# A hybrid attention trunk: new matmul tiles and a new order in the even mixer, and a new order around three other places

## The chip, the core and the metric

The kernel runs on one NeuronCore of a Trainium2 chip. The metric is the device time of one execution in microseconds (us). Before the change it is 1285.05 us, the median of three runs (1284.8, 1285.05 and 1287.28). Lower is better. TensorE is called PE here, VectorE DVE, ScalarE ACT, GpSimd POOL and SyncE SP.

## The reference

Two post-norm residual layers on x of 512 tokens by 1024 features, float32 throughout. The even layer runs gated linear attention (GLA, 4 heads) and local attention (8 query heads, 2 key heads, 64 features each) side by side. The odd layer is gated DeltaNet. Each mixer and each SwiGLU block is followed by a layer norm.

```python
def _even_mixer(x, w_in, w_a2, b_a, gla_norm_g, sinks, w_out):
    h = x @ w_in
    gq, gk, gv, ga, gr, sq, sk, sv = _split_cols(h, EVEN_WIDTHS)
    o = jnp.concatenate([_gla(gq, gk, gv, ga, gr, w_a2, b_a, gla_norm_g),
                         _swa(sq, sk, sv, sinks)], -1)
    return o @ w_out

# _swa: chunks of 64 tokens, each sees itself and the chunk before it
    sc = jnp.einsum('bcikgd,bcjkd->bckgij', qc, kw).astype(f32) * (SWA_HEAD_DIM ** -0.5)
    sc = jnp.where(valid[None, :, None, None, None, :], sc, -jnp.inf)
    ...
    p = jax.nn.softmax(jnp.concatenate([sc, sink], -1), axis=-1)[..., :-1]
    o = jnp.einsum('bckgij,bcjkd->bcikgd', p.astype(vw.dtype), vw)

# _gla, per chunk: attention within the chunk plus a state carried on
    attn = jnp.where(causal, jnp.einsum('bhcid,bhcjd->bhcij', q_g, k_g), 0.0)
    o_intra = jnp.einsum('bhcij,bhcjv->bhciv', attn, vc)
        o_c = jnp.einsum('bhid,bhdv->bhiv', q_c, state)
        state = state * jnp.exp(bl_c)[..., None] + jnp.einsum('bhjd,bhjv->bhdv', k_c, v_c)
    ...
    o = _norm_no_affine(o) * norm_g * jax.nn.silu(r)

# every sub-layer
    x = _layer_norm(ALPHA * x + mix, ln1_g[layer], ln1_b[layer])
```

## The kernel before, in words

Tokens are worked in four tiles of 128 (`NT` = 4, index t). All engines run hand-written programs, and their order is the order of the code. They meet by semaphores. The eight PSUM banks are handed out by `unit_plan`, which walks the list of all matmul units in PE's order and gives each the next bank of a ring. A unit waits in `fill` until the last user of its bank has `take`n the result.

Large products are split. A weight or an activation is rounded by ACT to a high part (`w_hi`, `x_hi`), and the rest (`w_lo`, `x_lo`) is subtracted by POOL or DVE. Each product then is three matmuls in fp32r (`mm3`, lines 1562 to 1564). Weights come in blocks of 1 MB through two buffers: SP loads one, ACT rounds it (`split_to`, line 768), POOL makes the low part (`split_lo`, line 638). The small products of the mixers are plain fp32, where one matmul is recorded as two passes.

In the even mixer, PE does for each tile t: scores of the local attention (line 1782, 64 tokens of a chunk by 128 keys, with keys padded by zeros to 128 features), two transposes of the decayed GLA keys (`kd`), the whole projection tile `gr` (24 matmuls of 512 columns), GLA products (`gattn` line 1794, `gstate` line 1771, `gout` lines 1762 and 1808), transposes of the probabilities (`probT`, line 1815), the local output (`sout`, line 1824), and transposes of the concatenated output of the tile before (`oT`, line 1695). DVE takes the maximum of the scores, subtracts it and writes `s_p` (line 1247). ACT takes the exponential of `s_p` (line 880), DVE sums it and scales the output. After the four tiles come tiles of the output projection, `mix`, of which two are placed ahead of the last `oT` (`TAIL_FILLERS`).

After each layer norm, `turn_x` (line 1680) transposes the normalised x into eight banks. DVE scales each bank into `f_ab` (line 1083), ACT rounds it (line 775), DVE and POOL in turn make `x_lo` (lines 1075 and 645). The first weight block behind it is walked with `fresh` set: for each k, two output banks, three matmuls each, after `x_lo` of k has come.

The odd layer convolves 24 channel blocks (`CONV_ORDER`, on DVE at line 1355) and then runs the delta rule over the four tiles. Projection tiles (`FILLERS`) are set between the small products. Its outputs are scaled by DVE (`out_scale`) and multiplied by the gate on POOL (`gate_output`, line 678) before they are turned.

## Time and profile before

| what | before |
|---|---|
| median of 3 runs | 1285.05 us |
| the profiled execution: its time, its span | 1283.91 us, 1282.1 us |
| PE busy, matmuls recorded | 1250.3 us (98%), 7104 |
| DVE, ACT, POOL busy | 462.7, 432.9, 598.9 us |
| mean DMA rate | 96 GB/s |
| even mixer's four tiles, PE | 94.39 to 159.80 us |

The span is the stretch between the first and last record, and the time of the execution lies 1.8 us above it. A busy engine is not always an engine at its peak: records of matmuls overlap, so the distance from one start to the next tells more than the length of one. Idle time is written in brackets behind a row, with the engine that ended it.

### The profile page before, as it was taken

What the parts mean: (1) busy time and instruction counts of PE and PEld (TensorE: products, weight loads), DVE (VectorE), ACT (ScalarE), POOL (GpSimd) and SP (SyncE); (2) the same over time, 40 slices, a digit from 0 to 9 for tenths busy, and PEclk for the clock granted to TensorE, in tenths of its full rate; (3) what the DMA queues carried; (4) which work ended last, traced back from release to release, by engine and by line L of the source; (5) the groups of instructions that cost most, each with busy time, mean ns of one, the idle gap of its engine ahead of it and who ended that gap; (6) DMA issues with size and microseconds to landing.
All of it is one profiled execution on the core that took longest, in us unless ns stands there. A gap on an engine that the chain in (4) does not pass through costs nothing.

```text
span 1282.1 us, 16970 instructions
## 1 busy us (share of the span) xinstructions
PE 1250.3 (98%) x7104; PEld 1027.5 (80%) x7104; DVE 462.7 (36%) x763; ACT 432.9 (34%) x600; POOL 598.9 (47%) x286
## 2 busy tenths in 40 slices
PE   9999999999999999998999999999999999999997
PEld 7878877888888888886777878887788888888885
DVE  5548945211111000115687955553521101010105
ACT  4174623322222221224453355452422222221111
POOL 4241243964444443445743346364595444435341
PEclk9999999999999999999999999999999999999999
DMA  9321032333333233231344342022233333324221
GB/s 305 99 67 66 1 115 84 99 99 99 98 99 99 83 121 125 99 96 49 98 110 124 99 100 92 26 67 99 66 99 99 99 99 99 99 82 134 80 99 65
DMA packets 109375, 122.98 MB, mean 96 GB/s; under 512 B 22386, under 2 KB 84148, under 8 KB 109300
## 3 DMA queue, kind: packets, MB, share of 16 engines
q1 hardware_dynamic: 101828, 118.59, 29.4%
q10 hardware_dynamic: 7472, 3.31, 1.0%
q8 instruction: 56, 0.92, 0.3%
q14 instruction: 19, 0.16, 0.0%
HBM read 117.96 MB, written 3.70 MB: 95 GB/s over the span
## 4 chain that ended last, share of the span: by engine, by line
PE 86%; DVE 7%; POOL 3%; issue 3%; DVEq 1%; ACT 1%; ACTq 0%; POOLq 0%
PE bank L1562 26%; PE bank L1563 26%; PE bank L1564 26%; PE bank L1893 3%; POOL w_lo L638 2%; DVE f_ab L1083 1%; DVE KH L1355 1%; DVE OO L1333 1%; DVE SS L1331 1%; PE bank L1608 1%; DVEq L435 1%; PE bank L1721 0%; PE bank L1845 0%; DVE x_tm L1106 0%; PE bank L1782 0%
## 5 line engine op out<-in xcount | busy, mean ns | idle before, releaser
L638 POOL TENSOR_TENSOR w_lo<-w_raw,w_hi 128x1024 fp32r<-128x1024 f32 (+1 forms) x200 | 470.0, 2374 | 495.3 <-ACT w_hi L768 495.3
L1562 PE MATMUL bank<-x_hi,w_hi 128*128 128x512 f32 x928 | 364.3, 393 | 7.5 <-DVE f_ab L1083 4.0
L1564 PE MATMUL bank<-x_hi,w_lo 128*128 128x512 f32 x928 | 361.7, 390 | 0.0
L1563 PE MATMUL bank<-x_lo,w_hi 128*128 128x512 f32 x928 | 361.6, 390 | 0.0
L768 ACT ACTIVATE w_hi<-w_raw 128x1024 fp32r<-128x1024 f32 (+1 forms) x200 | 196.3, 1031 | 218.3 <-issue 167.3
L1562 PEld LDWEIGHTS bank<-x_hi,w_hi 128*128 128x128 f32 x928 | 174.6, 188 | 46.9 <-issue 8.4
L1564 PEld LDWEIGHTS bank<-x_hi,w_lo 128*128 128x128 f32 x928 | 174.5, 188 | 36.6
L1563 PEld LDWEIGHTS bank<-x_lo,w_hi 128*128 128x128 f32 x928 | 174.5, 188 | 35.4
L1150 DVE TENSOR_TENSOR f_ab<-bank,f_ab 128x512 f32<-128x512 f32 x44 | 30.4, 691 | 368.9 <-PE bank L1564 368.9
L1563 PE MATMUL bank<-w_lo,h_hi 128*128 128x512 f32 x352 | 140.4, 399 | 0.0
L1562 PE MATMUL bank<-w_hi,h_hi 128*128 128x512 f32 x352 | 138.7, 394 | 0.0
L1564 PE MATMUL bank<-w_hi,h_lo 128*128 128x512 f32 x352 | 138.0, 392 | 0.0
L1562 PE MATMUL bank<-w_hi,x_hi 128*128 128x512 f32 (+1 forms) x320 | 124.3, 388 | 3.6 <-POOL w_lo L638 2.1
L1564 PE MATMUL bank<-w_hi,x_lo 128*128 128x512 f32 (+1 forms) x320 | 121.5, 380 | 0.0
L1563 PE MATMUL bank<-w_lo,x_hi 128*128 128x512 f32 (+1 forms) x320 | 121.3, 379 | 0.0
L1141 DVE SCALAR_TENSOR_TENSOR x_tm<-x_tm,bank 128x512 f32<-128x512 f32 x32 | 22.0, 687 | 260.9 <-PE bank L1564 259.7
L803 ACT ACTIVATE h_hi<-f_ab 128x512 fp32r<-128x512 f32 x44 | 27.8, 633 | 189.0 <-DVE f_ab L1150 189.0
L1562 PEld LDWEIGHTS bank<-w_hi,h_hi 128*128 128x128 f32 x352 | 66.1, 188 | 17.2
L1564 PEld LDWEIGHTS bank<-w_hi,h_lo 128*128 128x128 f32 x352 | 66.1, 188 | 15.8
L1563 PEld LDWEIGHTS bank<-w_lo,h_hi 128*128 128x128 f32 x352 | 66.1, 188 | 15.2
L798 ACT ACTIVATE f_ab<-bank 128x512 f32<-128x512 f32 x44 | 26.4, 600 | 144.1 <-PE bank L1564 143.9
L1562 PEld LDWEIGHTS bank<-w_hi,x_hi 128*128 128x128 f32 x320 | 60.2, 188 | 16.5 <-POOL w_lo L638 3.4
(270 smaller groups left out, 1179.5 us busy)
## 6 DMA issues: line engine op xcount, KB each, us to landing
w_raw<-ffn_w_gate_dram SPq DMA_DIRECT2D x22, 1024.0 KB, 5.3
w_raw<-ffn_w_up_dram SPq DMA_DIRECT2D x22, 1024.0 KB, 5.3
w_raw<-ffn_w_down_dram SPq DMA_DIRECT2D x20, 1024.0 KB, 5.0
w_raw<-od_w_in_dram SPq DMA_DIRECT2D x16, 1024.0 KB, 5.9
w_raw<-ev_w_in_dram SPq DMA_DIRECT2D x8, 1024.0 KB, 5.9
w_raw<-ev_w_out_dram SPq DMA_DIRECT2D x4, 1024.0 KB, 5.1
w_raw<-od_w_out_dram SPq DMA_DIRECT2D x4, 1024.0 KB, 5.1
x_fm<-x_fm_dram SPq DMA_DIRECT2D x8, 256.0 KB, 6.7
```

Of the source, the lines that this page charges most:

```text
L435: e.drain()
L638: pool.tensor_tensor(w_lo[:, b % 2, c], w_raw[:, b % 2, c], w_hi[:, b % 2, c].bitcast(F32), ALU.subtract).then_inc(w_lo_ready, 1)
L768: act.activation(w_hi[:, i % 2, c], w_raw[:, i % 2, c], ACT.Copy).then_inc(w_hi_ready, 1)
L798: take(act.activation(f_ab[:, j, :], bank(("gate", layer, f + j))[:, :], ACT.Silu), ("gate", layer, f + j))
L803: act.activation(h_hi[:, f + j, :], f_ab[:, 2 + j, :], ACT.Copy).then_inc(s["h_hi_ready"], 1)
L1083: take(dve.tensor_scalar(f_ab[:, k % 4, :], src, lnc[:, gcol + k:gcol + k + 1], lnc[:, gcol + 16 + k:gcol + 17 + k], ALU.mult, ALU.add), ( ...
L1141: take(dve.scalar_tensor_tensor(cols, cols, ALPHA, bank(key)[:, :], ALU.mult, ALU.add), key)
L1150: take(dve.tensor_tensor(f_ab[:, 2 + f % 2, :], bank(("up", layer, f))[:, :], f_ab[:, f % 2, :], ALU.mult), ("up", layer, f))
L1562: pe.matmul(out_ap, st[0], mv_[0], start=start, stop=False)
L1563: pe.matmul(out_ap, st[0], mv_[1], start=False, stop=False)
L1564: return pe.matmul(out_ap, st[1], mv_[0], start=False, stop=stop)
L1893: return pe.matmul(o, a, b_, start=True, stop=True)
```

## The change

Even mixer. Even query heads lie on partitions 0 to 63 and odd ones on 64 to 127, so the scores are products of 64 features in four 64 by 64 tiles of the array, into two banks (index e is the parity of the head). Keys are no longer padded with zeros: they are written twice, and two transposes per tile do what four did. ACT takes the exponential straight from the bank, with the maximum as bias, and its sum output gives the denominators; that is eight instructions of 128 columns in place of two of 512 on `s_p`. POOL multiplies the probabilities by the inverse sums. The local output is computed by features (`windowed`), so it needs no transpose. `gattn` is computed only within chunks, `gout` from it in 64-row tiles, and the state of two heads is updated by one DVE instruction. Mean and variance come from `bn_stats`. Probabilities of tile t are turned and used in tile t+1, between parts of `gr`, and the last tiles of `mix` are interleaved with them.

Elsewhere. Normalised x is signalled in halves; the `fresh` block starts with the matmuls that need only `x_hi`; POOL makes the first half of the next weight block before the low parts of x. The first two convolutions no longer restart the ring of banks, and the copy of `ba_fm` moves from DVE to ACT. In the odd layer the transposes at the start take other banks, a filler goes ahead of `vTM`, `qk` goes ahead of the small blocks, the blocks' DRAM scratch is laid out in two planes, and the last output is scaled and gated by one DVE instruction per head, with the fillers around it reordered.

```diff
+EVEN_FILLERS = [[("gr", t)] for t in range(NT)]
+LAST_FILLERS = {0: [("mix", 0, 0, 2)], 1: []}
+def turned(layer, t, i):
+    return ("sout", t) if (layer, i) == (0, 1) else ("oT", layer, t, i)
@@ unit_plan
-        u += [("score", t, 0), ("score", t, 1), ("kd", t), ("gr", t), ("gattn", t), ("gstate", t, 0), ("gout", t),
-              ("gstate", t, 1), ("probT", t, 0), ("probT", t, 1), ("sout", t)]
+        u += [("score", t, 0), ("score", t, 1), ("kd", t)] + EVEN_FILLERS[t]
         if t:
-            u += [("oT", 0, t - 1, 0), ("oT", 0, t - 1, 1)]
+            u += [("probT", t - 1, 0), ("probT", t - 1, 1), ("oT", 0, t - 1, 0), ("sout", t - 1)]
+        u += [("gattn", t), ("gstate", t, 0), ("gout", t), ("gstate", t, 1)]
-        if key == ("conv", CONV_ORDER[0]):
+        if key == ("ba_fm",):
             ring, turn = list(range(6)), 0
-            ring, turn = [0, 1, 2, 3, 6, 7, 4, 5], 0
+            ring, turn = [0, 6, 7, 1, 2, 3, 4, 5], 0
+        elif key[0] == "gstate" and key[2] == 1 and key[1]:
+            b = slots["probT", key[1] - 1, 0][0]
@@ SP: the odd layer's blocks
-        t_dram = nc.dram_tensor("t_blocks", (P, SB, 2, SB), F32).ap()
+        t_dram = nc.dram_tensor("t_blocks", (2, P, SB, SB), F32).ap()
@@ POOL
+                        pool.wait_ge(s["s_den_ready"], t + 1)
+                        for e in range(2):
+                            p = s_p[:, t % 2, e, :].rearrange("p (h n) -> p h n", h=4)
+                            den = s_den[:, t % 2, e:QH:2].unsqueeze(2).broadcast_to([P, 4, P])
+                            pool.tensor_tensor(p, p, den, ALU.mult).then_inc(s["s_weight"], 1)
                 if b in turned:
+                    pool.wait_ge(s["z_norm"], 2 * NT * turned[b])
+                    split_lo(b + 1, (0,))
                     low_parts(turned[b])
@@ ACT: even tile
+                if t:
+                    copy_probs(t - 1)
-                    act.activation(s_p[:, g, :], s_p[:, g, :], ACT.Exp).then_inc(s["s_prob"], 1)
+                    for j in range(4):
+                        h = 2 * j + e
+                        ins = act.activation(s_p[:, t % 2, e, j * P:(j + 1) * P], bank(("score", t, e))[:, j * P:(j + 1) * P],
+                                             ACT.Exp, bias=s_max[:, h:h + 1], scale=HD ** -0.5,
+                                             accum_out=s_den[:, t % 2, h:h + 1])
@@ DVE: layer norm
-                    dve.tensor_scalar(x_tm[:, t, :], x_tm[:, t, :], mv[:, t, 0:1], rstd[:, t:t + 1],
-                                      ALU.subtract, ALU.mult).then_inc(s["z_norm"], 1)
+                    for h in range(2):
+                        c = slice(h * 512, (h + 1) * 512)
+                        dve.tensor_scalar(x_tm[:, t, c], x_tm[:, t, c], mv[:, t, 0:1], rstd[:, t:t + 1],
+                                          ALU.subtract, ALU.mult).then_inc(s["z_norm"], 1)
@@ DVE: even tile
-                    take(dve.scalar_tensor_tensor(heads4(s_p[:, g, :]), k4(key), HD ** -0.5,
-                                                  across(s_max[:, hs], P), ALU.mult, ALU.subtract), key)
@@ DVE: last output of the odd layer
-                out_scale(NT - 1, hg)
+                for h in range(4 * hg, 4 * hg + 4):
+                    ins = dve.scalar_tensor_tensor(OO[:, h, :], OO[:, h, :], oms[:, h:h + 1],
+                                                   gate_s[:, NT - 1, h * P:(h + 1) * P], ALU.mult, ALU.mult)
@@ PE: fresh block
+                for k in range(KD) if fresh is not None else ():
+                    weights_there(b, k)
+                    pe.wait_ge(s["x_hi_ready"], KD * fresh + k + 1)
+                    x = xcols(k, ALL)
+                    for n in range(len(keys)):
+                        pe.matmul(ps[:, :], w[0], x[0], start=k == 0, stop=False)
+                        pe.matmul(ps[:, :], w[1], x[0], start=False, stop=False)
+                    low_part_there(pe, fresh, k)
@@ PE: even tile
-                            ins = pe.matmul(ps[c * CH:(c + 1) * CH, hh * P:(hh + 1) * P],
-                                            s_qT[:, h // 2, chunk * CH:(chunk + 1) * CH],
-                                            s_kT[:, 2 * g + h % 2, chunk * CH:chunk * CH + 2 * CH],
+                            ins = pe.matmul(ps[e][c * CH:(c + 1) * CH, j * P:(j + 1) * P],
+                                            s_qT[dims, j, chunk * CH:(chunk + 1) * CH],
+                                            s_kT[dims, j // 2, chunk * CH:chunk * CH + 2 * CH],
                                             start=True, stop=True)
-                tile_of(("gr", t))
+                tile_of(gr, 0, 3)
+                if t:
+                    turn_probs(t - 1)
+                    turn_o(0, t - 1)
+                tile_of(gr, 3, 6 if t < NT - 1 else 8)
+                if t:
+                    windowed(t - 1)
...
+            for k0 in (0, 2):
+                for key in TAIL_FILLERS[0]:
+                    tile_of(key, k0, k0 + 2)
+            turn_probs(NT - 1)
+            for key in TAIL_FILLERS[0]:
+                tile_of(key, 4, 6)
+            windowed(NT - 1)
```

On PE, an even tile before read like this, from its scores to the next tile's (the rows of `gr` and of `sout` that repeat are left out):

```order
L1782 MATMUL bank<-s_kT,s_qT 64x128 x16
L1789 MATMUL bank<-eye,g_kd 128x128 x2
...
L1794 MATMUL bank<-q_pad,g_k 128x128 x4
L1771 MATMUL bank<-g_v,g_kdt 64x128 x4
L1762 MATMUL bank<-g_S,q_pad 64x128 x4
...
L1808 MATMUL bank<-g_v,g_at 128x128 x4
L1815 MATMUL bank<-eye,s_p 128x128 x8
L1824 MATMUL bank<-s_vsh,s_pT 64x64
L1824 MATMUL bank<-s_v,s_pT 64x64
...
L1695 MATMUL bank<-eye,o_tm 128x128 x8
```

And after, for tile 1, where the dots stand for parts of `gr` (9, 9 and 6 matmuls) and for repeats:

```order
L1864 MATMUL bank<-s_kT,s_qT 64x128 x16
L1872 MATMUL bank<-eye,g_kd 128x128 x2
...
L1829 MATMUL bank<-eye,s_p 128x128 x8
L1756 MATMUL bank<-eye,o_tm 128x128 x4
...
L1842 MATMUL bank<-s_pT,s_vsh 64x2x64 x2
L1842 MATMUL bank<-s_pT,s_v 64x2x64 x2
...
L1886 MATMUL bank<-q_pad,g_k 64x64 x8
L1853 MATMUL bank<-g_v,g_kdt 64x128 x4
L1820 MATMUL bank<-g_S,q_pad 64x128 x4
...
L1906 MATMUL bank<-g_v,g_at 64x128 x8
```

The probabilities and the local output of the tile before now stand inside `gr`, half of the transposes of `o_tm` are gone, and `gattn` and the product with `g_at` come in eight matmuls of 64 rows out.

On ACT, an even tile before:

```order
L875 ACTIVATE g_kdt<-bank 128x256
L879 ACT_TABLE_LOAD
L879 ACTIVATE s_snk<-s_snk 128x4
L880 ACTIVATE s_p<-s_p 128x512
...
L882 ACT_TABLE_LOAD
L882 ACTIVATE g_r<-bank 128x512
L887 ACTIVATE s_pT<-bank 128x512 x2
L891 ACT_TABLE_LOAD
L891 ACTIVATE g_var<-g_var,eps 128x4
```

And after, tile 2, with its waits:

```order
L901 ACTIVATE s_pT<-bank 128x512 [waits bank_full4]
L901 ACTIVATE s_pT<-bank 128x512 [waits bank_full5]
L911 ACT_TABLE_LOAD
L911 ACTIVATE s_snk<-s_snk 128x4 [waits s_shift]
L919 ACTIVATE s_p,s_den<-bank,s_max 128x128 [waits bank_full0,s_weight,s_den_ready,bank_full1]
L919 ACTIVATE s_p,s_den<-bank,s_max 128x128 x3
L911 ACTIVATE s_snk<-s_snk 128x4 [waits bank_taken0,s_shift]
L919 ACTIVATE s_p,s_den<-bank,s_max 128x128 [waits bank_full1,s_weight,s_den_ready,bank_full2]
...
L930 ACT_TABLE_LOAD
L930 ACTIVATE g_r<-bank 128x512 [waits bank_full3]
```

The copies of the probabilities moved ahead of the exponentials, and the exponentials now hold the two score banks (0 and 1 in this tile) until they end. `gattn` and the first `gstate` of the tile are given the same two banks.

On PE, the first block behind a layer norm, before (the second one, in front of the convolutions) and then after:

```order
L1562 MATMUL bank<-x_hi,w_hi 128x512 [waits bank_taken0,x_lo_even,w_lo_ready]
L1563 MATMUL bank<-x_lo,w_hi 128x512
L1564 MATMUL bank<-x_hi,w_lo 128x512
L1562 MATMUL bank<-x_hi,w_hi 128x512 [waits bank_taken1]
```

```order
L1642 MATMUL bank<-x_hi,w_hi 128x512 [waits bank_taken6,x_hi_ready,w_lo_ready]
L1643 MATMUL bank<-x_hi,w_lo 128x512
L1642 MATMUL bank<-x_hi,w_hi 128x512 [waits bank_taken7]
L1643 MATMUL bank<-x_hi,w_lo 128x512
L1646 MATMUL bank<-x_lo,w_hi 128x512 [waits x_lo_even]
L1646 MATMUL bank<-x_lo,w_hi 128x512
L1642 MATMUL bank<-x_hi,w_hi 128x512 [waits x_hi_ready]
```

The matmuls with the low part of x stand last in each k, and a wait for the high part has taken the place of the first one.

## Rows read from the trace of the kernel before

**Rows 1.** The page: busy time of PE.
```profile
PE 1250.3 (98%) x7104; PEld 1027.5 (80%) x7104; DVE 462.7 (36%) x763; ACT 432.9 (34%) x600; POOL 598.9 (47%) x286
```

**Rows 2.** Waits of PE: engine, line, releaser: total us, times, longest us.
```profile
PE bank L1562 <- DVE f_ab L1083: 4.0, 2, 3.5
...
PE bank L1934 <- DVE KH L1355: 3.2, 1, 3.2
PE bank L1562 <- POOL w_lo L638: 2.1, 2, 1.1
...
PE bank L1893 <- DVE GA L1462: 1.6, 3, 0.5
...
PE bank L1782 <- ACT g_v L870: 0.9, 1, 0.9
```

**Rows 3.** Timeline of PE, even tile 1: start us, length us, instruction, records.
```profile
109.95 1.92 PE L1782 MATMUL bank<-s_kT,s_qT 128*64 128x128 f32 x32
111.80 0.44 PE L1789 MATMUL bank<-eye,g_kd 128*128 128x128 f32 x2
...
117.58 1.05 PE L1794 MATMUL bank<-q_pad,g_k 128*128 128x128 f32 x8
118.56 0.65 PE L1771 MATMUL bank<-g_v,g_kdt 64*64 64x128 f32 x8
119.14 1.09 PE L1762 MATMUL bank<-g_S,q_pad 128*64 128x128 f32 x8
...
123.01 1.04 PE L1815 MATMUL bank<-eye,s_p 128*128 128x128 f32 x8
...
125.59 1.09 PE L1695 MATMUL bank<-eye,o_tm 128*128 128x128 f32 x8
126.61 0.33 PE L1782 MATMUL bank<-s_kT,s_qT 128*64 128x128 f32 x2
```

**Rows 4.** Timeline of PE, odd layer: products in 32 by 32 tiles.
```profile
759.26 0.69 PE L1893 MATMUL bank<-blocks_in,GA 32*32 32x32 f32 x32
```

**Rows 5.** Timeline of ACT and DVE: nearest rows to the new instructions.
```profile
846.76 2.53 ACT L1009 ACTIVATE GT<-GT,ndec 128x128 f32<-128x128 f32 x8 [2.89 <-POOL GT L698]
849.31 1.28 ACT L993 ACT_TABLE_LOAD   x1
...
855.78 1.13 DVE L1502 SCALAR_TENSOR_TENSOR qkv<-bank,nbexp,qkv 128x128 f32<-128x128 f32 x4
...
126.10 0.69 DVE L1284 TENSOR_TENSOR r_tmp<-o_tm 128x512 f32<-128x512 f32 x1
...
159.19 1.28 DVE L1280 TENSOR_SCALAR g_mu<-g_mu 128x4 f32<-128x4 f32 x1
```

**Rows 6.** Timeline, behind the first and the second layer norm.
```profile
212.57 0.63 ACT L775 ACTIVATE x_hi<-f_ab 128x512 fp32r<-128x512 f32 x1 [0.84 <-DVE f_ab L1083]
...
214.14 0.47 PE L1562 MATMUL bank<-x_hi,w_hi 128*128 128x512 f32 x1 [1.69 <-DVE x_lo L1075]
...
582.15 0.63 ACT L775 ACTIVATE x_hi<-f_ab 128x512 fp32r<-128x512 f32 x1 [0.84 <-DVE f_ab L1083]
...
585.58 0.47 PE L1562 MATMUL bank<-x_hi,w_hi 128*128 128x512 f32 x1 [3.55 <-DVE f_ab L1083]
...
589.76 0.39 PE L1562 MATMUL bank<-x_hi,w_hi 128*128 128x512 f32 x1
```

**Rows 7.** Busy time by stretch; the eighth figure is the granted clock.
```profile
586.90:589.50 2.60, 2.44 (x6) 1.95 (x7) 1.92 (x4) 1.26 (x2) 1.32 (x2) 0.50 0.00 0
```

**Rows 8.** Timeline: the odd layer's constants on ACT's queue, and their use.
```profile
601.36 0.34 ACTq L934 DMA_DIRECT2D o_own<-c_small_dram  x1
...
607.86 0.51 PE L1867 MATMUL bank<-o_eye,ba_fm 128*128 128x16 f32 x4
```

**Rows 9.** Timeline of POOL: in the even mixer's last tile, and the last gate products.
```profile
155.74 9.86 POOL L638 TENSOR_TENSOR w_lo<-w_raw,w_hi 128x1024 fp32r<-128x1024 f32 x4
...
871.27 2.89 POOL L678 TENSOR_TENSOR OO<-OO,gate_s 128x512 f32<-128x512 f32 x2 [16.44 <-DVE OO L1436]
```

More of the change, by code:

```diff
@@ L871, in _, with copy_probs @@
             split_to(first_block[("gr",)] + 1)
+            def copy_probs(t):
+                for g in range(KVH):
+                    full(act, ("probT", t, g))
+                    take(act.activation(s_pT[:, g, :], bank(("probT", t, g))[:, :], ACT.Copy), ("probT", t, g))
             for t in range(NT):
@@ L1259, in _ @@
                     v = 2 * t + c
[L1260 to L1266 removed]
+                    col = (2 * t + c + 1) * CH - 1
@@ L1699, in have @@
                 def have(k):
[L1700 to L1703 removed]
+                    taken(pe, turned(layer, NT - 1, k // 4))
+                tm_group(("mix", layer, 1), have, in_turn=True)
                 turn_x(2 * layer + 1)
```

340 lines of the change are left out of this document (189 added, 151 removed).

## The prediction, made blind

> **What bounds the kernel now.** I read the page first: PE is busy for 98% of the span, the other engines for half of it or less [rows 1]. So only PE's queue counts: instructions taken out of it, a stretch in which it ran slowly, or a wait of its own. Another engine costs something only where PE waits for it. The list of PE's waits comes second. The ones that this change touches are short: 4.0 and 2.1 us before line 1562, 3.2 us for `KH`, 1.6 us for `GA`, 0.9 us for `g_v` [rows 2]. Third, I read the timeline of even tile 1, start to start, since lengths overlap [rows 3]. The tile takes 126.61 - 109.95 = 16.66 us. Scores take 1.85 (to 111.80). `kd` and the 24 matmuls of `gr` take 5.78 (to 117.58), so about 0.23 a matmul. `gattn` takes 0.98 and the first four `gstate` matmuls 0.58. From 119.14 to 123.01 lie 3.87 of GLA products with one wait, then 2.58 of `probT`, a wait for its copy, and `sout`, and 1.02 of `oT`. A group of four fp32 matmuls of 128 columns (8 records) takes 0.98: I read that as 4 x 0.213 plus 0.13 for the change of shape. `gstate`, which uses two column halves at once, costs 0.58 for the same count, half of 0.85 plus 0.13. A transpose is one record: `probT`'s eight and `kd`'s two give 0.10 to 0.11 each.
>
> **The even mixer, PE alone.** The new tile holds these parts. Scores: 16 matmuls. If the four 64 by 64 tiles run side by side they need 16 x 0.213 / 4 + 0.13 = 0.98; if only two do, today's 1.85. The trace has no 64 by 64 fp32 product in four tiles, so these are the bounds. The nearest row is the odd layer's products in 32 by 32 tiles: 32 records (16 matmuls of 32 columns, 16 x 0.053 + 0.13 = 0.98 in series) were over in 0.69 [rows 4], so tiles of different rows do overlap. I take 1.0. `kd` stays at 0.19, and `gr` costs 5.59 plus two more changes of shape, 5.85. `probT` 0.98. `oT` with four transposes in place of eight: 0.43 plus no change of shape behind `probT`. `windowed` 8 matmuls of 128 columns by halves, 0.98. `gattn` in chunks, eight of 64 columns by halves, 0.56, `gstate` 2 x 0.58, the products with `g_S` 2 x 1.02, `g_v` by `g_at` in eight 64-row matmuls 0.98. The sum is 14.2, against 16.66.
>
> The last term has a dissenter. Rows 4 show two row tiles going into one bank and overlapping, 0.69 against 0.98. The Trainium skill, "TensorEngine Tiling (Array Packing)", section Restrictions and Gotchas, says: "Different row tiles cannot access same PSUM bank simultaneously". By it the eight matmuls would stand in a row, 8 x 0.213 + 0.13 = 1.83, or 0.85 more in each tile and 3.4 in the four; the forecast would be 1269.4. The scores keep the rule, since each row half has its own bank.
>
> **The even mixer, the other engines.** PE will not reach 14.2, because `oT` and the scores' banks now hang on DVE and ACT. After a tile's last product DVE does its statistics, four scalings of 128 columns from a bank (1.13 for four of that kind) and a product of 512 columns (0.69) [rows 5]; with `bn_stats` on four heads, which I price like four more of 128 columns, and small operations (0.17 when nobody disturbs, 1.28 at worst, beside POOL's `w_lo` [rows 5]) `o_tm` is ready some 5.2 us into the next tile. PE, after scores, `kd`, 9 matmuls of `gr` and `probT`, wants it at about 4.4. Wait: 0.8. ACT copies the probabilities of the tile before until about 5.3, loads a table (1.28), and does eight exponentials at 2.53 / 8 = 0.32 [rows 5]: they end at about 9.6. `gattn` and the first `gstate` take the two score banks, which are only free then, and PE is there at about 9.3. That is another 0.3. The new tile is therefore 14.2 + 0.8 + 0.3 = 15.3, a gain of about 1.35 in tiles 1 and 2.
>
> Tile 0 starts 1.06 earlier, since nothing waits for `g_v` any more (0.9 in [rows 2], the rest the change of shape), and it carries neither `probT` nor `windowed` nor `oT`: 2.58 + 1.0 go out (3.37 of these 3.6 come back behind tile 3), with 0.5 to 0.6 saved by `gattn` and half the scores. I put tile 1's start at 105.0 instead of 109.95, which after the part that only moves leaves 1.6. With 1.35 twice and a little more for tile 3, whose scores and `gattn` give 1.3 as well, that is 7 us at its end. From there the tail counts: today PE resumes about 31.6 behind tile 3's start. Its pace is POOL's there, 9.86 / 4 = 2.47 per `w_lo` of 1024 columns [rows 9], for which PE already waits 1.1 at its longest [rows 2]; the change adds two products of 512 columns (about 1.25 each) to POOL in this place and `probT` and `windowed` to PE, covered by two `mix` tiles. I add 0.4. The even mixer so comes to **-6.5**, by the gains alone -9.4 at most, and 0 if each tile runs at the old pace. Two transposes of keys in each tile go away with the second half of `s_kT`, 8 x 0.106 in all: **-0.85**.
>
> **Layer norms.** Behind the first, PE starts at 214.14, while `x_hi` of k = 0 ended at 212.57 + 0.63 = 213.20 [rows 6]. The new order needs only that: -0.9, and 0.2 more since the next low part no longer holds it: **-1.1**. The third behaves alike: **-1.1**. Behind the second it is more. `x_hi` ended at 582.78, PE started at 585.58 (a bank of the ring was held by `f_ab`, 3.55 of idle time), then ran with a granted clock of 0.50, the lower level, in which six matmuls took 2.60 instead of 1.4 [rows 7], after a stretch in which it had been idle; the tenth matmul began at 589.76 [rows 6]. With the ring no longer restarted PE begins at about 582.8 at full clock and its tenth matmul is at about 585.0: -4.8. What is late next is the constants: ACT issues their load at 601.36 and PE uses them at 607.86, 6.5 behind [rows 8]; the use moves to about 602.9, and I let PE wait 1.3. **-3.5**, between 0 (if the whole of it waits for the load) and -4.8.
>
> **The odd layer.** The wait for `KH`, 3.2, falls away as the first transposes take banks whose users are long done; for this the scratch blocks must land 3 us earlier, and they are now written in long runs. The three waits for `GA`, 1.6, have `qk` placed in front. At the end POOL's two gate products, 2.89 [rows 9], leave the path; DVE does them per head with the scaling, four and four of 0.28, where it did a scaling of 0.69 twice: 0.8 more on DVE for 2.89 less on POOL, of which 1.1 reaches PE, since fillers cover the rest. **-5.9**, between -1 and -6.5.
>
> **Sum.** 6.5 + 0.85 + 1.1 + 1.1 + 3.5 + 5.9 = 18.95. The profiled execution took 1283.91 (span 1282.1 and 1.8 around it), which gives 1265.0. The median of the runs shown, 1285.05, is 1.1 above it, so I forecast **1266**. All terms at their good end give 1285.05 - (9.4 + 0.85 + 2.4 + 4.8 + 6.5) = 1261; with half of the even gain and half of the odd one it is about 1272, and with one more such loss 1274: own range 1261.5 to 1274.
>
> **Rivals.**
> A: the even mixer gains nothing. A tile is as long as the loop over DVE, ACT and the two shared banks. For it: POOL's new products stand on the same engine as `w_lo` (2.47 each), and a single small DVE operation has cost 1.28 beside it; four such make the loop 16.7. Or the scores need 1.85 and the sums a copy more. Against it: DVE and ACT are busy for a third of the span, and DVE's chain from the bank loses its passes of 0.69 over `s_p`. Then 6 go: 1272.
> B: the odd layer's loads set the time. If blocks or constants land no earlier, 3.2 of the `KH` wait stands again as a DMA wait, and the norm's gain shrinks by 0.5 more: 1269.7. For it: PE's need moves forward by 3 us and the issue doesn't. Against: the writes leave earlier too.
> C, slower: the sum output of the exponential. No row shows an exponential with one. It could cost a separate read behind each instruction, and 0.65 us more on each of 32 makes the ACT chain of a tile 8 x 0.65 = 5.2 longer. Since PE waits for the last exponential at `gattn`, all but nothing of that is covered: 4 x 5.2 = 21 turns 1266 into 1287. It decides from 19 / 32 = 0.6 on. If it is 0.3, the tile grows 2.4 and the result is about 1275. For it: eight outputs in place of none. Against: the nearest row, eight activations of this size, runs at 0.32 each with nothing between.
> D: all tiles at PE's own pace of 14.2, no wait for `o_tm`: 1.1 less in each of three, and the constants land in time: 1261.5.
>
> **Chances.** Forecast 0.58, A 0.22, B 0.10, C 0.05 (0.04 of it above 1282), D 0.05. My range for 8 times in 10 is 1259 to 1277: it takes in D with its bounds, A, B and the mild form of C. About 0.2%, 2.6 us, is what a measurement of this kernel can tell from no change. Faster by more 0.93; within it 0.03, which needs A with C's mild form and B; slower 0.04, C in full.
>
> **What the profile after would show.** Scores of a tile within about 1.0 us (wrong: 1.85). From one tile's scores to the next's 15.3 (A: 16.6; D: 14.2), with PE waiting for `o_tm` at line 1756 and for ACT at `gattn`. An exponential with sum at 0.32 (C: about 1.0, or an extra record behind each). The group of `g_v` by `g_at` at 0.98 (the quoted rule: 1.8). The first matmul behind the first and third layer norm 0.9 earlier relative to `x_hi`. Behind the second a granted clock of 1.0 and a start with `x_hi`; a wait for the constants' load at the product with `ba_fm`, 1.3 at most. No wait for `KH`; if one for a DMA is there, B. The forecast is wrong as a whole if even tiles are 16 us or longer, or if a wait of over 3 us appears in the odd layer that [rows 2] do not have.

## The result, and the profile after

The changed kernel takes 1275.43 us (median of four runs, 1275.22 to 1279.39); the kernel before, with one more run beside them, 1286.09. The ratio is 0.9925, 95% interval 0.9902 to 0.9948. The change is a gain of some 10 us, where 19 were forecast: 1275.4 against 1266, inside the stated range and outside the forecast's own (1261.5 to 1274). The profiled execution took 1275.52 us, its span is 1273.7.

The first look is at the same two views as before. The page:

```profile
PE 1241.7 (97%) x7080; PEld 1020.2 (80%) x7080; DVE 439.2 (34%) x768; ACT 440.6 (35%) x657; POOL 605.2 (48%) x292
```

PE is still the bound, but it is busy for 8.6 us less than in [rows 1] and the span is 8.4 shorter. So as much idle time came in as went out. The waits of PE say where (engine, line, releaser: total us, times, longest):

```profile
PE bank L1608 <- DVE KH L1398: 5.4, 1, 5.4
PE bank L1853 <- ACT s_p L919: 3.7, 3, 1.4
PE bank L1608 <- POOL w_lo L655: 3.1, 3, 2.5
PE bank L1642 <- ACT x_hi L799: 2.9, 3, 1.0
PE bank L1608 <- DVE x_lo L1138: 1.5, 2, 0.7
...
PE bank L1886 <- ACT s_p L919: 1.0, 2, 0.6
PE bank L1756 <- DVE OO L1581: 0.9, 2, 0.5
```

The waits of [rows 2] for `f_ab`, for `GA` and for `g_v` are gone. A wait for `KH` is there, but not the old one: it stands before line 1608, a large matmul of a convolution. Three others are new, two for the exponentials `s_p` and one for `x_lo` in front of line 1608. The wait for `x_hi`, 2.9 in all at the three norms, stands where one for `x_lo` was before (3.4 in all at two of them).

A table by stage follows, read from the starts of single matmuls in the two timelines (us). The rest of the analysis goes by it.

| stage of PE | before | after | measured | forecast |
|---|---|---|---|---|
| start to first scores | 94.39 | 93.95 | -0.44 | with the next |
| even mixer, to the first turn of x | 113.26 | 112.24 | -1.02 | -7.35 for both |
| first norm and up projection | 246.37 | 245.85 | -0.52 | -1.1 |
| down projection | 123.21 | 120.86 | **-2.35** | 0 |
| second norm, to the product with `ba_fm` | 30.63 | 26.58 | -4.05 | -3.5 |
| convolutions, to the first `kTM` | 134.00 | 138.28 | **+4.28** | -3.2 |
| delta rule, output projection | 161.80 | 160.12 | -1.68 | -2.7 |
| third norm and up projection | 246.37 | 245.88 | -0.49 | -1.1 |
| down projection | 123.36 | 121.01 | **-2.35** | 0 |

Three places are off, in both directions: the even mixer, the convolutions, and two stages in which the diff changes nothing.

**The convolutions.** The timelines of PE and then of DVE around the new wait:

```profile
655.51 0.46 PE L1935 MATMUL bank<-qkv 128*32 128x32 f32 x32
661.40 0.80 PE L1608 MATMUL bank<-x_hi,w_hi 128*128 128x512 f32 x1 [5.43 <-DVE KH L1398]
661.99 0.63 PE L1609 MATMUL bank<-x_lo,w_hi 128*128 128x512 f32 x1
```
```profile
650.28 1.28 DVE L1439 TENSOR_SCALAR ssq<-ssq 128x32 f32<-128x32 f32 x1
...
651.98 1.94 DVE L1441 TENSOR_TENSOR beta<-beta,rk 128x32 f32<-128x32 f32 x1
...
655.25 1.28 DVE L1450 TENSOR_TENSOR GT<-GT,nbeta 128x512 f32<-128x512 f32 x2
656.62 4.72 DVE L1398 SCALAR_TENSOR_TENSOR KH<-bank,convw,KH 128x511 f32<-128x511 f32 x6
```

DVE works through a list of small operations and comes only at 656.62 to the two convolutions that PE has finished last (three instructions each). PE wants the bank of the second of them at once, and gets it at 661.34. After that its granted clock is down to the lower level, 0.59 of full speed on average over 5.6 us (the eighth figure):

```profile
661.40:667.00 5.60, 5.60 (x15) 4.50 (x16) 0.00 (x0) 0.10 (x1) 3.92 (x2) 0.59 0.13 16
```

The 24 large matmuls behind the wait take 7.80 where the neighbouring groups of 24 take 5.66, so the wait costs 5.43 + 2.14 = 7.6 us. Why there, `unit_plan` tells. The ring of six banks now starts at `ba_fm`, two units later than before, so the twelfth convolution of `CONV_ORDER` gets bank 0. The thirteenth restarts the ring of four, and gets bank 0 too. Before, the twelfth had bank 2.

**Even tiles.** PE at the start of tile 1, in its middle, and at the start of tile 2 (the two records of a product are counted apart, and a few stand in rows of their own that are left out):

```profile
105.13 0.97 PE L1906 MATMUL bank<-g_v,g_at 64*64 64x128 f32 x13
...
106.00 1.09 PE L1864 MATMUL bank<-s_kT,s_qT 64*64 64x128 f32 x30
107.03 0.44 PE L1872 MATMUL bank<-eye,g_kd 128*128 128x128 f32 x2
...
114.44 0.69 PE L1886 MATMUL bank<-q_pad,g_k 128*64 128x64 f32 x16 [0.38 <-ACT s_p L919]
116.44 0.65 PE L1853 MATMUL bank<-g_v,g_kdt 64*64 64x128 f32 x8 [1.32 <-ACT s_p L919]
...
122.10 1.09 PE L1864 MATMUL bank<-s_kT,s_qT 64*64 64x128 f32 x30
123.13 0.44 PE L1872 MATMUL bank<-eye,g_kd 128*128 128x128 f32 x2
124.30 0.50 PE L1608 MATMUL bank<-w_hi,x_hi 128*128 128x512 f32 x1 [0.74 <-DVE x_lo L1138]
```

The products themselves cost what was forecast: scores 1.03 (1.0), `g_v` by `g_at` in 64-row tiles 0.87 up to the scores (0.98; 1.02 in e6, where another shape follows), in one bank, on different halves of its partitions, and side by side; in series they would have been 1.7 to 1.83. So the dissenting term of the prediction, 1.83 by the quoted rule, did not come: this measurement decides against it. But tile 1 is 16.10 long and tile 2 17.39 (forecast 15.3, and 16.66 in [rows 3]), with waits for the exponentials of 1.7 and 2.1 where I had 0.3 (0.9 in tile 3), and in tiles 2 and 3 one of 0.74 for `x_lo` in front of `gr`, which I had not at all. Behind tile 3 PE waits 2.48 for POOL's `w_lo`, and the granted clock over the next 3.0 us is 0.53:

```profile
154.39 1.09 PE L1906 MATMUL bank<-g_v,g_at 64*64 64x128 f32 x16
157.96 0.77 PE L1608 MATMUL bank<-w_hi,x_hi 128*128 128x512 f32 x1 [2.48 <-POOL w_lo L655]
```

On ACT a read of the accumulator stands behind each exponential, 0.345 from one exponential to the next:

```profile
112.88 0.37 ACT L919 ACTIVATE s_p<-bank,s_max 128x128 f32<-128x128 f32 x1
113.14 0.19 ACT L919 ACTIVATION_READ_ACCUMULATOR s_p<-bank,s_max 128x1 f32 x1
113.24 0.36 ACT L919 ACTIVATE s_p<-bank,s_max 128x128 f32<-128x128 f32 x1
```

**Down projection.** The first matmul of the stage and the one behind its last, before and then after:

```profile
454.02 0.39 PE L1562 MATMUL bank<-w_hi,h_hi 128*128 128x512 f32 x1
...
577.23 0.27 PE L1680 MATMUL bank<-eye,x_tm 128*128 128x128 f32 x1
```
```profile
452.04 0.39 PE L1608 MATMUL bank<-w_hi,h_hi 128*128 128x512 f32 x1
...
572.90 0.27 PE L1742 MATMUL bank<-eye,x_tm 128*128 128x128 f32 x1
```

The same 528 matmuls, with no wait inside, start every 0.2333 us before and every 0.2289 after. The instructions are the same. The granted clock is 1.00 in both. What moved is their data: the even mixer's small buffers grew by 32 bytes in each partition, and everything allocated behind them, h included, now starts at a multiple of 64 bytes instead of 32 beyond one. That this is the cause is not shown by these rows; e1, e2 and others below try it.

### The profile page after: what moved, and what is told of

It is laid out like the page before. It is cut to its first block, busy times and chain, and to the rows that moved or that the text cites. A ratio compares the mean times of both kernels' runs of the same rounds, so it can differ in the third digit from the quotient of the medians.

```text
span 1273.7 us, 17029 instructions
## 1 busy us (share of the span) xinstructions
PE 1241.7 (97%) x7080; PEld 1020.2 (80%) x7080; DVE 439.2 (34%) x768; ACT 440.6 (35%) x657; POOL 605.2 (48%) x292
## 4 chain that ended last, share of the span: by engine, by line
PE 89%; DVE 5%; ACT 2%; POOL 2%; DVEq 1%; issue 1%; ACTq 0%; POOLq 0%
PE bank L1608 27%; PE bank L1609 26%; PE bank L1610 26%; PE bank L1983 3%; POOL w_lo L655 1%; PE bank L1646 1%; DVEq L449 1%; PE bank L1642 1%; PE bank L1643 1%; DVE stats L1190 1%; ACT s_p L919 1%; DVE x_tm L1188 1%; DVE x_tm L1161 1%; PE bank L1667 1%; PE bank L1780 1%
## 5 line engine op out<-in xcount | busy, mean ns | idle before, releaser
L1608 PE MATMUL bank<-x_hi,w_hi 128*128 128x512 f32 x880 | 345.3, 392 | 5.4 <-DVE KH L1398 5.4
L1609 PE MATMUL bank<-x_lo,w_hi 128*128 128x512 f32 x880 | 343.3, 390 | 0.0
L1610 PE MATMUL bank<-x_hi,w_lo 128*128 128x512 f32 x880 | 343.2, 390 | 0.0
L1608 PEld LDWEIGHTS bank<-x_hi,w_hi 128*128 128x128 f32 x880 | 165.7, 188 | 40.9 <-DVE KH L1398 5.5
L1610 PEld LDWEIGHTS bank<-x_hi,w_lo 128*128 128x128 f32 x880 | 165.7, 188 | 34.5
L1609 PEld LDWEIGHTS bank<-x_lo,w_hi 128*128 128x128 f32 x880 | 165.8, 188 | 34.2
L1610 PEld LDWEIGHTS bank<-w_hi,h_lo 128*128 128x128 f32 x352 | 66.1, 188 | 14.8
```

The source lines that it names most:

```text
L1608: pe.matmul(out_ap, st[0], mv_[0], start=start, stop=False)
L1609: pe.matmul(out_ap, st[0], mv_[1], start=False, stop=False)
L1610: return pe.matmul(out_ap, st[1], mv_[0], start=False, stop=stop)
```

## The experiments

They were timed in four groups, each beside the kernel before, whose median there was 1285.25, 1285.08, 1285.07 and 1284.95.

**e3, the ring of the convolutions.**

```diff
         elif key == ("conv", CONV_ORDER[BLOCKS_AT]):
-            ring, turn = list(range(4)), 0
+            ring, turn = [1, 2, 3, 0], 0
         elif key == FILLERS[0, -1]:
-            ring, turn = [0, 6, 7, 1, 2, 3, 4, 5], 0
+            ring, turn = [1, 6, 7, 2, 3, 0, 4, 5], 0
```

> The changed kernel with one thing different: the ring of four banks for the last twelve convolutions starts at bank 1 and not at 0 (and the ring behind it is turned the same way). In the changed kernel conv 11 and conv 12 in order both have bank 0, and PE waits 5.4 us there and then runs at the lower clock for a while. Theory R (ring collision): the wait goes, the 7.6 us lost between the 12th and the 13th convolution come back, about 1268. Rival (DVE bound): DVE's queue of small operations in front of conv 11 is what is late; PE then waits one or two convolutions later for another bank, and less than 2 us are gained.

Measured: 1267.21 us (1267.1 to 1267.68), ratio to before 0.9858 [0.9842, 0.9873]. The stage from `ba_fm` to `kTM` goes from 138.28 to 130.65, 7.63 less, and no other stage moves by more than 0.1; the start to the first scores, which the edit doesn't touch, varied by 0.8 between these two executions and gives the rest. Behind the same small products PE now goes on at once:

```profile
654.77 0.46 PE L1935 MATMUL bank<-qkv 128*32 128x32 f32 x32
655.16 0.50 PE L1608 MATMUL bank<-x_hi,w_hi 128*128 128x512 f32 x1
```

DVE's list was no shorter, and PE waits for none of it later. So the cause is the shared bank, not DVE's load: the theory of the ring collision.

**e4, the banks of the even tiles.** Each unit of a tile gets a role, and the roles change banks from tile to tile. `probT` of the tile before has E and F, its `oT` G, its `sout` H. One more line, not shown, restarts the ring behind the tiles.

```diff
+        even.update({("score", t, 0): roles["A"], ("score", t, 1): roles["B"], ("kd", t): roles["C"],
+                     ("gr", t): roles["D"], ("gattn", t): roles["E"], ("gstate", t, 0): roles["F"],
+                     ("gout", t): roles["C"], ("gstate", t, 1): roles["E"]})
+        roles = {x: roles[y] for x, y in zip("ABCDEFGH", "EFABDGHC")}
```

> The changed kernel with the banks of the even mixer's tiles handed out by hand: gattn and the first gstate take the banks of the turned probabilities, not those of the scores, and gr no longer takes the bank of the oT of the tile before. Theory B (banks): of the waits in tiles 1 to 3 (1.7, 0.9 and 2.1, 0.9 and 1.1 us) most go, tiles 1 and 2 come to 14.5 to 15 us instead of 16.1 and 17.4, and the kernel gains 3 to 5. Rival (latency): the wait moves to the turning of the probabilities, because POOL scales them only behind g_r at the end of the tile before, and under 1.5 us is gained.

Measured: 1270.93 us (1270.19 to 1271.65), ratio 0.9885 [0.9872, 0.9899], 4.5 less than the changed kernel. The even mixer's stage goes from 112.24 to 107.08. PE from the start of tile 1, in tile 2, and at the start of tile 3:

```profile
105.92 1.09 PE L1875 MATMUL bank<-s_kT,s_qT 64*64 64x128 f32 x30
106.94 0.44 PE L1883 MATMUL bank<-eye,g_kd 128*128 128x128 f32 x2
...
120.03 1.09 PE L1875 MATMUL bank<-s_kT,s_qT 64*64 64x128 f32 x30
121.06 0.44 PE L1883 MATMUL bank<-eye,g_kd 128*128 128x128 f32 x2
...
123.41 1.04 PE L1840 MATMUL bank<-eye,s_p 128*128 128x128 f32 x8
125.05 0.65 PE L1767 MATMUL bank<-eye,o_tm 128*128 128x128 f32 x4 [0.61 <-DVE o_tm L1349]
...
134.87 1.09 PE L1875 MATMUL bank<-s_kT,s_qT 64*64 64x128 f32 x30
```

Tile 1 is 14.11 long, at PE's own pace (worked out as 14.2), and tile 2 14.84, with a wait for `o_tm` of 0.61, which the prediction had at 0.8. So the engines' chains were sized about right, and theory B holds: the banks made the tiles long. In the changed kernel `gattn` and the first `gstate` stand in the banks of their own tile's scores, and `gr` of tiles 2 and 3 in the bank of the `oT` that was made one tile earlier, which is held until `x_lo` is written from it.

**e5, both tables.** The edits of e3 and e4 together.

> The changed kernel with both bank tables (the last twelve convolutions from bank 1, and the even mixer's tiles by hand). The two places are 440 us apart and share nothing, so if each gain is what it was alone (8.2 and 4.5 us) the sum is 12.7: about 1262.7. Rival: an earlier start of the later stages meets late DMAs of weights (the buffers come free earlier, but SP issues at its own times) and 2 or more of it is lost, 1265.

Measured: 1262.42 us (1262.23 to 1262.74), ratio 0.9824 [0.9810, 0.9837]. The two gains add (13.0 less than the changed kernel, 8.2 and 4.5 alone), and PE waits for no DMA.

**e6, the first weights of `mix` rounded earlier.** On top of e5, on ACT in tile 3:

```diff
+                if t == NT - 1:
+                    split_to(first_block[("mix", 0, 0)])
                 if t:
                     round_o(0, t - 1)
```

> As e5, and ACT rounds the first half of the output projection's first weights (two instructions of 1024 columns, 2.0 us) ahead of the gate's sigmoid product in the last even tile, so that POOL can make its low part earlier. Theory W: the wait of 2.6 us for w_lo behind the last even tile and the stretch at a granted clock of 0.57 behind it go; 2.5 to 3.5 us less than e5, about 1259.5. Rival: ACT is the late one there, g_r and with it POOL's scaling come 2 us later, and PE waits as long for the turned probabilities; within 1 us of e5.

Measured: 1259.32 us (1258.74 to 1259.86), ratio 0.9799 [0.9786, 0.9813], 3.1 less than e5. The even mixer's stage is 103.58, after 107.07. PE goes from tile 3 into `mix` at once, at full pace, where e4 and e5 still had the wait of 2.6:

```profile
148.76 1.09 PE L1919 MATMUL bank<-g_v,g_at 64*64 64x128 f32 x16
149.78 0.50 PE L1621 MATMUL bank<-w_hi,x_hi 128*128 128x512 f32 x1
150.12 0.40 PE L1622 MATMUL bank<-w_lo,x_hi 128*128 128x512 f32 x1
```

So POOL wasn't the late one, as my tail term had it: in the changed kernel it had been idle for 13.8 us before its first `w_lo` here, waiting for `w_hi`.

**e8, the second norm alone.** The kernel before with only its ring changed.

```diff
-        if key == ("conv", CONV_ORDER[0]):
+        if key == ("ba_fm",):
             ring, turn = list(range(6)), 0
         elif key == ("conv", CONV_ORDER[BLOCKS_AT]):
-            ring, turn = list(range(4)), 0
+            ring, turn = [1, 2, 3, 0], 0
         elif key == FILLERS[0, -1]:
-            ring, turn = [0, 1, 2, 3, 6, 7, 4, 5], 0
+            ring, turn = [1, 2, 3, 0, 6, 7, 4, 5], 0
```

> The kernel before with nothing but the ring of banks in front of the convolutions: it is no longer restarted for conv 0 but two units later, and the last twelve convolutions start at bank 1, so that no two neighbours share a bank. Theory N (the second norm's wait is that restart): the idle 3.7 us behind the second layer norm come down to the 1.85 of the other two norms, and the stretch at the lower clock goes; 3 to 3.5 us faster than before, 1282. Rival: without the new order of the first block nothing is gained there, because PE needs the low part of x, and under 1.5 us come out.

Measured: 1281.98 us (1281.03 to 1283.77), ratio 0.9976 [0.9967, 0.9985]. The stage of the second norm goes from 30.63 to 27.21, 3.42 of the 4.05 that the whole change gives there. Theory N. The wait for the constants' load that the prediction looked for is small: 0.28 in this run, and none in the changed kernel.

**e11, the low part first.** On top of e5, the fresh block in its old order of matmuls.

```diff
-                        pe.matmul(ps[:, :], w[1], x[0], start=False, stop=False)
-                    low_part_there(pe, fresh, k)
-                    for n in range(len(keys)):
-                        ins = pe.matmul(bank(keys[n])[:, :], weights(b, k, n * P, P)[0], x[1], start=False, stop=k == KD - 1)
+                        if n == 0:
+                            low_part_there(pe, fresh, k)
+                        pe.matmul(ps[:, :], w[0], x[1], start=False, stop=False)
+                        ins = pe.matmul(ps[:, :], w[1], x[0], start=False, stop=k == KD - 1)
```

> As e5 (both bank tables), but the first block behind each layer norm again takes its three matmuls per bank in the old order, with the wait for the low part of x ahead of them. By the prediction's step this gives back 0.9 to 1.1 per norm, so 3 us slower than e5 (1265.4). What the trace after shows speaks for less: PE starts 0.9 earlier but then waits 0.4 for the low part, which leaves 0.5 a norm, 1.5 us (1264).

Measured: 1269.36 us (1267.27 to 1270.45), ratio 0.9874 [0.9859, 0.9889]: 6.9 more than e5, where the two workings gave 3 and 1.5. In the profiled run the three norms cost 2.5, 3.9 and 1.0 more than in e5. Behind the first, PE waits for the low part, and then runs at a granted clock of 0.52 over 3.4 us:

```profile
203.97 2.22 PE L1753 MATMUL bank<-eye,x_tm 128*128 128x128 f32 x16 [0.38 <-DVE x_tm L1172]
208.60 0.76 PE L1655 MATMUL bank<-x_hi,w_hi 128*128 128x512 f32 x1 [2.42 <-DVE x_lo L1131]
```

The old order waits 1.7 there in the kernel before [rows 6] and 2.4 here, since DVE's first low part takes 1.25 beside POOL's `w_lo`, not 0.68, and the lower clock was in neither working.

**e7, POOL's order.** On top of e5, POOL makes the low parts of x first again, and the next block's behind them.

```diff
-                split_lo(b, (1,) if b - 1 in turned else (0, 1))
+                split_lo(b)
...
-                    pool.wait_ge(s["z_norm"], 2 * NT * turned[b])
-                    split_lo(b + 1, (0,))
                     low_parts(turned[b])
```

> As e5, but POOL again makes the low parts of x first behind each layer norm and the first half of the next weight block after them. Theory C (contention): in the changed kernel POOL's w_lo of 2.37 us runs beside DVE's first x_lo, which takes 1.27 instead of 0.68, and delays POOL's own x_lo; without it the first low part is 0.6 earlier and each norm gives 0.3 to 0.6 us back, 1 to 1.5 us less than e5. Rival: the low part of the next block is then late for PE (a wait of 0.2 stood there before) and e7 is equal to e5 or up to 1 us slower.

Measured: 1264.51 us (1263.95 to 1266.84), ratio 0.9843 [0.9830, 0.9857], 2.1 more than e5. My theory had the mechanism, and for the whole kernel the wrong sign. DVE's low part is back at 0.68 and the wait of 0.23 for it is gone, but the next weights come too late for the second block:

```profile
207.00 1.30 POOL L673 TENSOR_TENSOR x_lo<-f_ab,x_hi 128x512 fp32r<-128x512 f32 x1 [11.52 <-ACT x_hi L808]
...
214.51 1.29 POOL L673 TENSOR_TENSOR x_lo<-f_ab,x_hi 128x512 fp32r<-128x512 f32 x1 [1.25 <-ACT x_hi L808]
215.76 4.74 POOL L666 TENSOR_TENSOR w_lo<-w_raw,w_hi 128x1024 fp32r<-128x1024 f32 x2
```

The first of these is done at 218.1, and PE starts its second block at 218.19, after a wait of 0.9; the stage is 0.76 longer at both SwiGLU blocks, and the second norm's 0.44. The new orders of POOL and PE work as a pair: the one makes the low part later, the other lets PE work meanwhile.

**e12, sums by DVE.** On the changed kernel, the exponentials without the sum output, and two reductions on DVE.

```diff
-                                             accum_out=s_den[:, t % 2, h:h + 1])
@@ DVE
+                for e in range(2):
+                    link(dve.tensor_reduce(s_den[:, t % 2, e:QH:2], heads4(s_p[:, t % 2, e, :]), AX, ALU.add))
```

> The changed kernel (no bank table of mine), with the exponentials' sum output left off and the sums taken by two reductions of DVE per tile, as before. The trace shows a read of the accumulator behind each exponential, but the next one starts 0.345 us after the one before, against 0.316 for a row of this size without. If the sum output costs just that, ACT's eight are 0.25 earlier per tile, PE waits as much less, and the kernel is 0 to 0.8 us faster; if DVE's 1.4 us more per tile hold anything up it is up to 1.5 slower. Rival C of the prediction (0.65 for each) would make this kernel about 15 us faster than the changed one.

Measured: 1272.81 us (1272.42 to 1273.75), ratio 0.9907 [0.9893, 0.9920], 2.6 less than the changed kernel, of which the even mixer's stage has 2.1 (112.24 to 110.13). Four exponentials now come in one run:

```profile
113.04 1.14 ACT L919 ACTIVATE s_p<-bank,s_max 128x128 f32<-128x128 f32 x4
```

1.14 / 4 = 0.285 each, against 0.345 with the read, and 1.55 from one group of four to the next against 1.91: 0.09 an exponential, the small instruction between the groups included. Rival C had its mechanism (a read of its own) and a price seven times too high. The eight exponentials of a tile end 0.72 earlier so; three tiles wait for them, which makes 2.2, and the stage gave 2.1. I had expected at most 0.8, because I took one without a sum at 0.316.

**e1, e2, e9, e10, e13, e14, places in SBUF.** Unused bytes in front of an allocation move everything behind it. e1 is the kernel before, e14 is e6, and the others are the changed kernel.

```diff
+        here[0] += 32     # e1, e2; in e14 64
         ARENA = here[0]   # h and the mixers' buffers
@@ e9: w alone, so 32 again ahead of x; e13: the first line only
+        here[0] += 32
         w_hi = sb("w_hi", [P, 2, WCOLS], F32R)
         w_lo = sb("w_lo", [P, 2, WCOLS], F32R)
+        here[0] += 32
         x_hi = sb("x_hi", [P, KD, SEQ], F32R)
@@ e10: x alone, so 32 ahead of x_hi and 32 again behind x_lo
```

Expected, in this order:

> The kernel before, with 32 bytes of unused space ahead of the arena in SBUF, so that h_hi, h_lo, qkv and the mixers' buffers start at multiples of 64 bytes as they do in the changed kernel (before they start 32 bytes off). Theory P (placement): the matmuls of the down projection, whose stationary operand is h, start every 0.2333 us before and every 0.229 after; with the padding they go at 0.229 and the kernel is 4 to 4.5 us faster than before (about 2.1 in each SwiGLU block). Rival: the pitch comes from something else in the change (POOL's or ACT's order, DMA), then this kernel stays within 0.5 us of before.

> The changed kernel with the same 32 bytes of padding, which undoes the alignment. Theory P: 4 to 4.5 us slower than the changed kernel (about 1279.7), with a pitch of 0.2333 in the down projection, and the gain over before shrinks to about 6. Rival: no change.

> The changed kernel with w_hi and w_lo alone moved to a start 32 bytes off a multiple of 64 (everything else stays aligned). In the up projection the weights are the stationary operand and x moves, in the down projection h is stationary and the weights move. Theory S: a stationary operand that starts off by 32 bytes makes each matmul of its stage start 2% later; the up stages (246 us each, two of them) and the odd projections grow by 4 to 5 us each, 10 us slower than the changed kernel, and the down stages stay at 121. Rival M: it is the moving operand; the down stages go from 121 to 123.3 and the up stages stay at 245.9. Rival 0: only h's own place counts, nothing changes.

> The changed kernel with x_hi and x_lo alone moved 32 bytes off. They move in the up projection and are stationary in gr, mix and og. Theory S: up stages stay at 245.9; the even mixer and the tail of the odd layer grow, by 2% of their 512-column matmuls, 2 to 3 us in all. Rival M: up stages grow by about 5 us each, to 251.

> The changed kernel with everything behind w_raw moved by 32 bytes: w, x and h all start 32 off a multiple of 64, so the two operands of each large matmul stand alike. Theory R (relative place): a matmul is slow where one operand is off and the other is not; here up stages stay at 245.9 and down stages at 120.9, and the kernel is within 1 us of the changed one. Theory A (absolute place): any operand that is off by 32 costs; up stages go to 252.7 or more and down to 123.2 or more, 20 us slower or worse.

> As e6 (both bank tables and the earlier rounding, 1259.3), with the arena moved by 64 bytes, so that h stays a multiple of 64 but stands 64 later against w, as it did in e10, whose down stages took 119.7 instead of 120.9. Theory H: the distance between h and w counts beyond the multiple of 64; down stages 119.7, 2.3 us less in all, 1257. Rival: e10's short down stages came from something of its own (x off by 32), and this kernel equals e6 within 0.5 us.

Measured, with the start of w, x and h in bytes beyond a multiple of 64, the distances in bytes from the start of w to those of h and x modulo 128 (worked out from the allocations), and the first pair of stages as in the table above:

| kernel | w, x, h | h - w, x - w | norm and up | down | median us |
|---|---|---|---|---|---|
| before | 0, 0, 32 | 32, 0 | 246.37 | 123.21 | 1285.25 |
| e1 | 0, 0, 0 | 64, 0 | 246.39 | 120.86 | 1282.71 |
| after | 0, 0, 0 | 64, 0 | 245.85 | 120.86 | 1275.43 |
| e2 | 0, 0, 32 | 96, 0 | 245.86 | 123.19 | 1280.30 |
| e9 | 32, 0, 0 (x and h 64 later) | 96, 32 | 252.69 | 123.21 | 1305.64 |
| e10 | 0, 32, 0 (h 64 later) | 0, 32 | 252.69 | 119.71 | 1299.24 |
| e13 | 32, 32, 32 | 64, 0 | 245.86 | 120.86 | 1276.49 |
| e14 | 0, 0, 0 (h 64 later) | 0, 0 | 245.86 | 119.69 | 1256.93 |

Up works on w and x, down on w and h. A stage is slow exactly when one of its operands is 32 off and the other is not, whichever of them moves; with both off it is as fast as with none (e13). Theories S, M and A fall, the theory of the relative place (R in e13) holds. And the multiple of 64 isn't all: with h another 64 bytes later the down stage takes 1.15 less, in two kernels (theory H). Read by the distance modulo 128, all rows agree: at 0 down takes 119.7 and up 245.9, at 64 down takes 120.86 (+1.0%), at 32 or 96 down takes 123.2 (+2.9%) and up 252.69 (+2.8%). This reading was made after the runs, other distances weren't tried, and why the distance counts stays open. In the profile of e13 the down stage from its first to the matmul behind it:

```profile
451.37 0.39 PE L1609 MATMUL bank<-w_hi,h_hi 128*128 128x512 f32 x1
...
572.23 0.38 PE L1743 MATMUL bank<-eye,x_tm 128*128 128x128 f32 x2
```

and in that of e9, where the granted clock in both stages was 1.00 as well:

```profile
466.64 0.39 PE L1610 MATMUL bank<-w_hi,h_hi 128*128 128x512 f32 x1
...
589.85 0.38 PE L1744 MATMUL bank<-eye,x_tm 128*128 128x128 f32 x2
```

e9 and e10 lost 30 and 24 us, where 10 at most had been expected of each. The two norm and up stages give 13.7 of it, and the down stages of e9 4.7. Their even mixers took 119.4 and 119.5 in place of 112.24, of which the operands' places explain some 3.1 at most (2.8% of the stage, an estimate). The clock has a part in the rest: in e9, PE waits 1.31 for the exponentials in tile 1, as in the changed kernel (1.32), but its granted clock is 0.50 from 118 to 124, where the changed kernel's is 1.00. One of e10's five executions had a mean granted clock of 0.994 and took 1294.4, the four others 0.989 and 1299.2 to 1299.7.

e1 gained 2.5 us (ratio 0.9975 [0.9965, 0.9984]) where its down stages gave 4.7. In its profiled execution the second norm's stage is 0.8 longer than before, and the delta rule's stage 2.8: behind the old wait for `KH` PE ran at 0.50 of its clock in this execution and at full clock in that of the kernel before (the eighth figure; e1, then before):

```profile
740.00:744.00 4.00, 4.00 (x14) 3.52 (x15) 3.97 (x3) 3.74 (x7) 4.00 (x3) 0.50 0.31 46
```
```profile
741.00:745.00 4.00, 3.14 (x18) 2.77 (x19) 3.96 (x4) 2.97 (x6) 4.00 (x3) 1.00 0.13 13
```

The wait is 3.2 long in both. It need not be a difference of the kernels: of e1's nine executions six had a mean granted clock of 0.992 (1282.5 to 1283.1 us) and three 0.994 or 0.995 (1281.1 to 1281.9), and of the 13 of the kernel before beside them three had 0.993 or 0.994 (1287.2 to 1287.5) where the ten others had 0.995 or 0.996 (1284.3 to 1285.6). What decides whether the clock falls stays open. e14, at 1256.93 us (1256.63 to 1257.37, ratio 0.9781 [0.9768, 0.9794]), is the fastest version that I ran, 18.5 below the changed kernel.

## Why the prediction was wrong

- **Where it failed: "The wait for `KH`, 3.2, falls away" and "With the ring no longer restarted PE begins at about 582.8".** Both came about (there is no such wait, and PE begins at 583.1 on that scale), and both come from new starts of the ring of banks. I followed the new ring at the two places where it removes a wait, and not to its next restart, at the thirteenth convolution, where it gives two neighbours one bank. That is 7.6 us, undone in e3 by the start of one ring. Without it the convolutions and the delta rule give 5.0, where I had 5.9: the convolutions 3.3 for 3.2, the delta rule and what follows it 1.7 for 2.7.
- **Even mixer, -7.35 forecast, -1.5 measured: the term "That is another 0.3" for the score banks, and no term at all for the bank of `gr`.** The terms of PE and of the chains held: with other banks tile 1 is 14.1 and tile 2 14.8 (e4), and the stage is at -6.2 (-7.1 with the start, which varied from 93.2 to 94.9 over all runs). I had found one shared bank (`gattn` on the scores) and gave it 0.3; it cost 1.7, 2.1 and 0.9 in tiles 1 to 3. The exponentials of tile 1 end 10.3 us into the tile, not 9.6, and PE is there at 8.1, not at 9.3: it waited 0.8 less for `o_tm`, and the rest is a slip of the prediction, whose own parts add up to some 8.8 there. I had not found the other (`gr` on `oT`, 0.74 of idle time in each of tiles 2 and 3). Tile 0 gave less than forecast too: tile 1 starts at 106.0, not at 105.0. With these, rival A was close in size to what happened, by the ring and not by POOL or the scores.
- **The tail, +0.4 forecast.** Its size was off, and its cause: PE waits 2.48 there, and e6 shows that the time of ACT's rounding sets it, not POOL's pace. With that moved the kernel is 3.1 faster, and the even mixer's stage at -9.7.
- **Norms.** The second came close to the forecast (-4.05 for -3.5), by the bank, but in part by luck: the tenth matmul gained 4.0, not 4.8, and the 1.3 that I took off for the constants did not come, as they were in time. The first and third gave half of the 1.1. PE starts 0.84 earlier against `x_hi`, but `x_hi` comes 0.23 later behind the first turn of x; then PE loses 0.4 to a low part that POOL's new order made later, and gains 0.2 at the second block, whose weights are in time. That neither order could have been left out (e7, e11) the prediction didn't see.
- **Down projections, 0 forecast, -4.7 measured.** No step of mine looked at where buffers lie. The change brings in `neg_sinks`, doubles `s_den` and drops `g_mu`. Without this gain the result is 1280.3 (e2), outside the stated range: that the measured time lies inside it is luck.
- **Right:** PE as the bound, the cost of the new products in tiles, two row tiles in one bank side by side (0.87 us for eight matmuls), no late load of blocks (rival B), a cheap sum output (rival C at 0.09 for 0.65).

The forecast of 1266 was missed by 9.4: two losses of 7.6 and 5.2, both from the table of banks, met one gain of 4.7, and the smaller misses of the tail, the first and third norm and the delta rule make the rest.

## What to carry to other kernels

Where a table or a ring hands out buffers, write the new assignment out for the whole program and look for neighbours that share one, above all at each restart: a change that shifts the ring by two units moves every wait behind it. A wait that goes at one place is only gained if the same edit brings none at another. And when stages change their pace that nobody edited, compare the addresses of their operands before any other cause.

## What the runs showed of the hardware

- Of the starts of a 512-column matmul's two operands in SBUF the distance counted. With 32 or 96 bytes of it modulo 128 the down projection took 123.2 us, with 64 120.86 and with 0 119.7; norm and up took 252.69 with 32 and 245.86 with 0.
- Eight fp32 matmuls in 64 by 64 tiles, four in each row half, into one bank and there on different halves of the partitions, took 0.87 to 1.02 us together, where in series an estimated 0.213 each [rows 3] would give 1.7.
- A sum output added 0.09 us to an exponential of 128 columns (1.91 for four in place of 1.55), with a record of its own.
- A subtraction of 512 columns on DVE from SBUF (`x_lo`) took 1.27 in place of 0.68 beside POOL's `w_lo` of 2.37. In e5 it began 0.72 before the end of that instruction and ended 0.55 behind it, so it may have stood still until then.
- Behind idle times of 5.4, 2.5 and 2.4 us PE ran at the lower of its two clock levels (1.2 and 2.4 GHz) for a while: the granted clock was 0.59, 0.53 and 0.52 over the next 5.6, 3.0 and 3.4 us. Behind one of 3.2 us it did so in the profiled execution of e1 and not in that of the kernel before, and behind one of 1.3 in that of e9 and not in that of the changed kernel.
